# Triangular inversions of a hybrid decoder: four 64x64 corners of TensorE, and the copies back split between ScalarE and VectorE

## What is computed

```
# RWKV-7, per head (16 heads, 64 wide)
S = S * w_t + sa[..., None] * (kk_t * a_t) + v_t[..., None] * k_t      # sa = S @ -kk_t
o_t = S @ r_t

# gated DeltaNet, per head (8 heads, 128 wide), per chunk of 64
Lmat = where(strict, (kb @ k.T) * decay, 0)
sol  = solve_triangular(Lmat + eye(64), rhs, unit_diagonal=True)
```

## Time and profile before

| | us |
|---|---|
| median of three runs | 2955.32 (2954.40 to 2958.49) |
| span of the profiled execution | 2958.0 |
| TensorE matmul busy | 2588.5 (88%) |
| weight loads busy | 2117.4 (72%) |
| VectorE busy | 1706.3 (58%) |
| ScalarE busy | 1469.3 (50%) |
| GpSimd busy | 358.2 (12%) |
| L770, V products (64x128 forms, two groups) | 91.3 + 42.1 |
| L765, F products (two groups) | 56.4 + 28.8 |
| L2223, masks, 144 of 424 ns | 61.1 |
| L1596, copies back, 144 of 597 ns | 57.3 + 28.7 |

### The profile page before, as it was taken

One profiled execution on the slowest core, in us unless ns is written; L12 is line 12 of the kernel. 1 busy time (PEld: TensorE's weight loads), 2 busy tenths in 40 slices (PEclk: granted clock), 3 DMA queues, 4 the chain that ended last, 5 costly groups with the idle time before them and its releaser, 6 DMA issues.

```text
span 2958.0 us, 67158 instructions
## 1 busy us (share of the span) xinstructions
PE 2588.5 (88%) x29799; PEld 2117.4 (72%) x29818; DVE 1706.3 (58%) x1983; ACT 1469.3 (50%) x1911; POOL 358.2 (12%) x180
## 2 busy tenths in 40 slices
PE   7988988899797989897988999787898898998986
PEld 6766666777465768665666777557888888888875
DVE  2445463234215542545462233128999999999996
ACT  2233343233224331433343233137888889888885
POOL 0000001000000000000001000001323243324231
PEclk9999999999998999998989999898999999999999
DMA  6411120123216634301121133237999999999994
GB/s 201 135 41 47 31 86 29 37 93 114 95 62 228 202 119 139 100 30 31 58 63 32 58 107 100 100 125 289 388 386 386 386 386 388 382 386 390 385 387 183
DMA packets 304032, 531.34 MB, mean 180 GB/s; under 512 B 18528, under 2 KB 145760, under 8 KB 303360
## 3 DMA queue, kind: packets, MB, share of 16 engines
q1 hardware_dynamic: 303600, 525.99, 50.3%
q10 hardware_dynamic: 144, 1.05, 0.1%
HBM read 524.91 MB, written 2.10 MB: 178 GB/s over the span
## 4 chain that ended last, share of the span: by engine, by line
PE 53%; DVE 33%; ACT 7%; issue 6%; DMA 0%; ACTq 0%; DVEq 0%; SPq 0%
DVE arena L2713 24%; PE bank L799 11%; PE bank L700 9%; PE bank L770 4%; PE bank L1277 4%; PE bank L1236 4%; PE bank L765 3%; PE bank L718 2%; DVE yacc L2721 2%; PE bank L1293 2%; PE bank L644 2%; PE bank L1025 1%; ACT arena L1897 1%; PE bank L875 1%; PE bank L1030 1%
## 5 line engine op out<-in xcount | busy, mean ns | idle before, releaser
L2713 DVE TENSOR_TENSOR arena<-ring,arena 128x2048 bf16<-128x2048 f32 x336 | 833.4, 2525 | 3.8 <-ACT arena L2012 3.8
L2012 ACT ACTIVATE arena<-ring 128x2048 bf16<-128x2048 f32 x336 | 640.4, 1911 | 98.9 <-DMA ring<-in_moe_w_down 30.2
L1378 PE MATMUL bank<-arena 128*128 128x0 bf16 x10752 | 490.6, 209 | 99.4 <-DVE arena L2713 96.3
L1378 PEld LDWEIGHTS bank<-arena 128*128 128x128 bf16 x10752 | 478.6, 100 | 113.7 <-DVE arena L2713 105.3
L799 PE MATMUL bank<-feat,ring 128*128 128x256 f32 x1664 | 433.6, 399 | 8.4 <-ACT ring L1575 2.3
L1527 POOL TENSOR_TENSOR arena<-yacc,arena 128x512 bf16<-128x512 f32 x112 | 300.2, 2692 | 1004.5 <-ACT arena L2035 1004.5
L799 PEld LDWEIGHTS bank<-feat,ring 128*128 128x128 f32 x1664 | 308.6, 196 | 87.3 <-issue 43.1
L1395 PEld LDWEIGHTS bank<-arena 128*128 128x128 bf16 x5376 | 237.8, 98 | 23.0 <-issue 20.0
L1395 PE MATMUL bank<-arena 128*128 128x0 bf16 x5376 | 245.0, 206 | 7.3 <-issue 3.8
L700 PE MATMUL bank<-feat,ring 128*128 128x256 f32 x1056 | 236.8, 388 | 7.7 <-issue 5.7
L700 PEld LDWEIGHTS bank<-feat,ring 128*128 128x128 f32 x1056 | 205.7, 195 | 38.2 <-ACT feat L1566 8.9
(11 more groups left out here) (355 smaller groups left out, 3434.5 us busy)
## 6 DMA issues: line engine op xcount, KB each, us to landing
ring<-in_moe_w_gate SPq DMA_DIRECT2D x112, 1024.0 KB, 8.4
ring<-in_moe_w_up SPq DMA_DIRECT2D x112, 1024.0 KB, 7.9
ring<-in_moe_w_down SPq DMA_DIRECT2D x112, 1024.0 KB, 8.4
ring<-in_w_in SPq DMA_DIRECT2D x76, 1024.0 KB, 5.2
ring<-in_xa_w_kv SPq DMA_DIRECT2D x16, 1024.0 KB, 5.3
ring<-in_ffn_w_gate SPq DMA_DIRECT2D x11, 1024.0 KB, 5.4
ring<-in_ffn_w_up SPq DMA_DIRECT2D x11, 1024.0 KB, 5.4
ring<-in_ffn_w_down SPq DMA_DIRECT2D x11, 1024.0 KB, 7.0
```

Of the source, the lines that this page charges most:

```text
L1378: m = mm(o, w[k // 4][wi][:, k % 4, col:col + P], xg[:, e % 2, xi, k, :].shape_from_register(width[e % 2]), start=i == 0 and k == 0, stop= ...
L2012: sc.activation(w_parts[b][0], ring[:, b * FFN_SLOT:(b + 1) * FFN_SLOT], ACT.Copy).then_inc(S["w_hi"], 1)
L2713: v.tensor_tensor(w_parts[b][1], ring[:, b * FFN_SLOT:(b + 1) * FFN_SLOT], w_parts[b][0], ALU.subtract).then_inc(S["w_lo"], 1)
```

## The change

It touches `invert` and the two `inverted`, and adds two helpers and one semaphore, `inv_VX`.

- V of a set is split. Its quarters 0 and 1 (straight) stay in bank 4+i, in the first 256 columns. Quarters 2 and 3 (crossed) go to the upper 256 columns of bank 2+i, above F, and to the other half of the partitions: rows h of the array give columns 1-h.
- TensorE loads the straight halves of both sets first, then waits for `inv_W` (VectorE reads the same bank) and loads the crossed halves.
- A level first does F of both sets, yields, and then V of both sets, and yields. Within V the quarters come in the order 0, 2, 1, 3. V waits for `inv_W`, which by then is the mask of the next level; F waits for both copies.
- ScalarE copies the straight part (128x256) and the half of the crossed part that goes to partitions 0 to 63 (64x256); VectorE copies the other half (64x256). ScalarE's waits for its own copy before are gone. Its yields stand behind the copies of both sets, VectorE's behind the masks of both sets and behind the copies of both sets.
- The last copies to `xt_` are eight of 64x128 a call in place of four of 64x256.

```diff
+        def inv_halves(i):
+            return (bk(4 + i, 0, T).rearrange("p (a b) -> p a b", a=2), bk(2 + i, T, T).rearrange("p (a b) -> p a b", a=2))
+        def inv_v(i, q, h):
+            straight, crossed = inv_halves(i)
+            return straight[HALF[h], q] if q < 2 else crossed[HALF[1 - h], q - 2]
...
-                    mm(bk4(4 + i)[:, :, 64:P], C("ident"), b4(C("eye2")), start=True, stop=True, skip_group_check=True)
+                    straight, _ = inv_halves(i)
+                    mm(straight[:, :, 64:P], C("ident"), b4(C("eye2"), 2), start=True, stop=True, skip_group_check=True)
                     for h, p_ in enumerate(HALF):
-                        m = mm(bk4(4 + i)[p_, :, 0:64], C("eye2")[p_], nt[h], start=False, stop=True, skip_group_check=True)
+                        mm(straight[p_, :, 0:64], C("eye2")[p_], nt[h][:, 0:2], start=False, stop=True, skip_group_check=True)
+                for i, (nt, xt_, vu, w) in enumerate(sets):
+                    _, crossed = inv_halves(i)
+                    pe.wait_ge(S["inv_W"], c.need("inv_W"))
+                    mm(crossed[:, :, 64:P], C("ident"), b4(C("eye2"), 2), start=False, stop=True, skip_group_check=True)
+                    for h, p_ in enumerate(HALF):
+                        m = mm(crossed[HALF[1 - h], :, 0:64], C("eye2")[p_], nt[h][:, 2:4], start=False, stop=True, skip_group_check=True)
                     m.then_inc(S["inv_V"], 1)
                 for b in range(LEVELS):
                     last = b == LEVELS - 1
                     for i, (nt, xt_, vu, w) in enumerate(sets):
-                        pe.wait_ge(S["inv_W"], c.need("inv_W"))
                         pe.wait_ge(S["inv_VU"], c.need("inv_VU"))
+                        pe.wait_ge(S["inv_VX"], c.need("inv_VX"))
                         if not last:
...
-                        f = slice(64 * last, P)
-                        for q in range(4):
+                    yield 0
+                    f = slice(64 * last, P)
+                    for i, (nt, xt_, vu, w) in enumerate(sets):
+                        if not last:
+                            pe.wait_ge(S["inv_W"], c.need("inv_W"))
+                        for q in (0, 2, 1, 3):
                             for h, p_ in enumerate(HALF):
-                                m = mm(bk4(4 + i)[p_, q, f], w[p_, b % 2, 64 * q:64 * q + 64], vu[p_, q, f], start=False, stop=True, skip_group_check=True)
+                                m = mm(inv_v(i, q, h)[:, f], w[p_, b % 2, 64 * q:64 * q + 64], vu[p_, q, f], start=False, stop=True, skip_group_check=True)
                         m.then_inc(S["inv_V"], 1)
-                        yield i
+                    yield 1
...
# ScalarE
                 for b in range(LEVELS):
                     for i, (nt, xt_, vu, w) in enumerate(sets):
+                        straight, crossed = inv_halves(i)
                         act.wait_ge(S["inv_V"], c.need("inv_V"))
-                        act.wait_ge(*c.last())
-                        sc.activation(vu, bk4(4 + i), ACT.Copy).then_inc(*c.inc("inv_VU"))
-                        yield i
+                        sc.activation(vu[:, 0:2], straight, ACT.Copy).then_inc(*c.inc("act_step"))
+                        sc.activation(vu[HALF[0], 2:4], crossed[HALF[1]], ACT.Copy).then_inc(*c.inc("inv_VU"))
+                    if b:
+                        yield 1
+                    yield 0
...
# VectorE
+                    if b or not corners:
+                        yield 0
+                    for i, (nt, xt_, vu, w) in enumerate(sets):
+                        _, crossed = inv_halves(i)
+                        dve.wait_ge(S["inv_V"], c.need("inv_V"))
+                        v.tensor_copy(vu[HALF[1], 2:4], crossed[HALF[0]]).then_inc(*c.inc("inv_VX"))
+                        dve.wait_ge(*c.last())
+                    if b or not corners:
+                        yield 1 if b else 0
```

14 lines of the change are left out of this document (9 added, 5 removed).

## The result

| | median, us | runs | ratio to the kernel before |
|---|---|---|---|
| before, on the same chip | 2954.86 | 2950.37 to 2958.49 | |
| after | 2926.19 | 2920.76 to 2929.78 | 0.9897 [0.9882, 0.9913] |

A forecast was written before the change was run, and what follows sets the result against it. TensorE was 53% of the chain that ended last, and the twelve `invert` calls 546 us. Second RWKV +3.6, first RWKV -22.4, first DeltaNet -25, second DeltaNet -8.4 gave -52: 2903 us, range 2878 to 2950.

The forecast's parts named there:

- Do four corners run at once: V products on TensorE: four records, one per array corner, were taken to run in each 0.109 us step.
- V's price: TensorE's V products in each level: forecast to fall from 0.87 to 0.44 us per set.
- Rival A: Crossed corners run no faster, V stays 0.87 us a set: 2953 us, no change; chance 0.08.
- Step (1): TensorE's levels in each call: 4.2 us in place of 5.1, -4.5 a call; the last level -0.6.
- the DeltaNet calls: First DeltaNet calls, with front steps of four heads beside: -12.5 us each, -25 for two.
- the one hand-over of 6.74 us: First RWKV calls, from the mask behind front step 3 to VectorE's step 4: 6.74 to 2.8 us, -3.9.
- Step (2): Start of a call, loads halved in columns: +0.7 us, and +0.3 since set 1's first F waits for copies.
- Step (3): ScalarE's split copies: 0.67 us a set with 0.10 overlap; eight copies to XT at the call's end, +0.4.
- Step (5): Second RWKV calls: piece after V waits for bank 7, emptied after V's copies; three times 1.5, +4.5 us a call.
- Step (4): V waits for the next level's mask; the 1.06 us piece covers it unless the mask queues behind VectorE front steps.
- Rival B: V's mask wait decides at every level of the six calls with front steps: 3001 us; chance 0.12.
- C: Front steps keep half their idle in first RWKV and first DeltaNet calls: -27, 2928 us; chance 0.20.

The follow-up runs named there:

- e3: Kernel before with the new order F, F, yield, V, V, yield alone, ScalarE's waits for its own copy dropped, V on two corners; 2897.23 us, ratio 0.9794.
- e9: e3 with V of each level but the last waiting for the next level's mask, F no longer for its own; 2917.20 us, ratio 0.9871.
- e2: Kernel after, but the crossed half of V and U stays on its own partitions, so only two diagonal corners work; 2957.95 us, ratio 1.0004.
- experiment 1: Kernel after, but ScalarE takes the side piece in its own turn in the eight RWKV calls, emptying bank 7 before V's copies; 2897.37 us, ratio 0.9810.

## Why the prediction was right in direction and 23 us too low

Four prices, each by one difference of two kernels, divide the result: the order alone -60 (e3 against before), V's wait for masks +20 (e9 against e3), split copies and longer starts +41 (e2 against e9), four corners -32 (after against e2). Counted in the twelve calls alone they are -53, +23, +31 and -28. They form a chain from before to after, so that they must add up to the whole (-31, measured -28.7 on one chip) whether or not each cause is rightly named; and a price depends on its place in the chain, as the corners show (-32 with the late evacuation, -41 without).

That the time fell inside the range of 2878 to 2950 was in part luck. Most of the largest gain, that of the order, was missing in the sum, and so was most of the loss by the mask wait and the split copies; as measured the two nearly cancel (-60 against +61).

- **Do four corners run at once, and V's price: right.** 0.49 a set with its step to the next, 1.03 for both, level 4.23. Rival A falls by e2.
- **Step (1), a level is -0.9: right in size, incomplete in what it names.** It counted the order as neutral (F, F, piece, V, V, piece, "as many changes of shape"). The order was the main gain. The forecast saw that only in the DeltaNet calls (-25, measured -29.8) and in the one hand-over of 6.74 us, which came out as forecast, 2.8 us (VectorE, the mask and its step 4; the earlier trace rows before):

```profile
178.00 0.88 DVE L2252 TENSOR_TENSOR arena<-bank,cs 128x256 f32<-128x256 f32 x2
...
180.81 0.69 DVE L2330 TENSOR_TENSOR arena<-bank,cs 128x512 f32<-128x512 f32 x1 [0.65 <-PE bank L898]
```

- **Step (2), start +1.0: right at full clock** (145.94 to the first F at 150.32 is 4.38, and 3.40 with the order alone), too low in the second RWKV calls: 5.56 in the one at 195.40, at a clock of 0.75 (experiment 1 has the row), and 4.39 in the same call of experiment 1, at 1.00.
- **Step (3), 0.67 for a set's copies: failed.** 0.79, inside the bounds of 0.60 to 0.80 but not at the value that the sum used. The overlap that L1993 and L1985 show is there between copies that stay on their partitions (e2, 0.28 apart) and not where one moves to the other half (0.41). The eight copies to XT start 0.295 apart for lengths of 0.27, where the forecast had 0.18 apart, and the next work waits 1.17 us for them, where the forecast had +0.4:

```profile
231.81 0.68 PE L998 MATMUL bank<-arena 64*64 64x64 f32 x16 [1.17 <-ACT arena L1629]
```

- **Step (5), the stall: right in place, cause and count, mis-sized.** Forecast 4.5 a call, or 18; taking it away gave 30.1. Each is 1.76 or 1.85, not 1.5, because of step (3); in the calls of the second group the last one falls at the end of the call (2.79 us). The idle time that went is 20.3 us, near the 18; the other 9.8 are TensorE's work at a clock of 0.89 to 0.97, which no term had and of which a part follows other waits (experiment 1). The 30.1 are 12 of the 18 us by which the second RWKV calls missed. The other 6 are there without the stall too (experiment 1, a call): 0.8 more of waiting for XT than forecast, 0.43 for the last copies ahead of V, 0.35 in the first level.
- **Step (4), V waits for the mask: named, and costed at nothing in the sum.** This is the step that failed in the first RWKV calls: two levels in each, 0.65 to 4.07 us each, 25 us by e9. That is more than the 10 us by which these calls missed, since the order gained more there (-42.7) than the forecast gave the whole change (-22.4). Rival B had the mechanism and wanted it at every level of six calls; it comes at two of five, in four calls. The text said "unless the mask is queued behind VectorE front steps" and could have counted them: masks that stand behind steps 1 and 3.
- **The clock was in no term.** Before the change the first RWKV calls ran at 0.90 to 0.97 (the sums of the earlier trace rows don't show it), with the order alone at 1.00; a third of that kernel's gain there (14.7 of 42.7 us) is shorter work of TensorE, and a third of the price of the mask wait (8.6 of 25.2) longer work.
- **C named the time (2928) and half the reason**: the first RWKV calls kept all of their idle time (40.8 us before, 44.5 after), the first DeltaNet calls did not (25.1, then 6.2).

## To carry to other kernels

Split a change of order and a change of mapping, and time them apart: here the order was worth twice the whole, and the mapping took half of it back except in the calls where TensorE alone set the pace. The mapping that saved matmul time by writing to other partitions was paid in the copies back, which got narrower and lost their overlap, and in the wait that the shared PSUM bank forced; count each wait against what is queued ahead of the releasing instruction on its engine, level by level. And when turns are regrouped, check every buffer whose release rides on those turns: moving one evacuation by one turn was worth as much as the change itself.

## What the hardware showed unexpectedly

- ScalarE's activations without a wait between them start 0.28 us apart (length 0.38) where both keep their partitions, 0.41 apart where one reads partitions 64 to 127 and writes 0 to 63. The Trainium skill (ScalarE: Activation LUTs, section "What ACT_TABLE_LOAD costs") states an overlap of about 93 ns for activations one behind another; the first pair agrees, the second does not. The 64x128 copies to XT, which go from one half of the partitions to the other by turns, don't overlap either (0.295 apart, length 0.27), in after, where half of them move, nor in e2, where each keeps its own partitions. So moving is not the only thing that ends the overlap.
- TensorE fills four 64x64 corners also when four calls on the diagonal corners stand ahead of the crossed ones (1.09 us for two sets, 1.03 with the corners mixed).
- What a wait of TensorE costs in the clock behind it differs with the wait. In the first RWKV calls of e9 it is 8.6 us of longer work for 16.6 of added idle time: the granted clock is 0.83 in the 10 us behind a wait of 3.44 us and 1.00 in the 6 us behind one of 2.03. In the kernel after it stays at 1.00 behind the three stalls of 1.76 to 1.85 us of the call at 195.40, and falls behind one such stall of the call at 331.23.
